# One written-out job order per engine for the even layer of a two-layer hybrid diffusion backbone

## The reference

```python
def even_inputs(h, w_in, lb, qn_w, kn_w):
    qa, zf, zb, ia, ga, qb, kb, vb = split_cols(h @ w_in, EVEN_SIZES)
    q_r = rec(jax.nn.silu(qa), DK_A) * (DK_A ** -0.5)
    g_f = jnp.log(lbf[0] + (1.0 - lbf[0]) * jax.nn.sigmoid(rec(zf, DK_A)))   # g_b from zb likewise
    v_r, gate = rec(ia, DV_A), ga.reshape(b, l, H_A, DV_A)
    q_a = rms_norm(qb.reshape(b, l, H_B, HD_B), qn_w)
    k_a = rms_norm(kb.reshape(b, l, KV_B, HD_B), kn_w)
    v_a = vb.reshape(b, l, KV_B, HD_B)

def even_layer_lat(h, p, j, lbs, k_ctx, v_ctx, s_ctx):     # the context tokens likewise
    o_r, _ = hgrn_bidir(q_r, g_f, g_b, v_r, s0[:, 0], s0[:, 1])        # mixer A, 4 heads
    out_a = hgrn_readout(o_r, gate, p['hgrn_norm_w'][j])               # rms_norm(o) * silu(gate)
    out_b = swa_latent_attention(rope_2d(q_a), rope_2d(k_a), v_a, k_ctx, v_ctx, p['swa_sink'][j])
    return jnp.concatenate([out_a, out_b], -1) @ p['w_out_even'][j]
```

## Time and profile before

| | |
|---|---|
| median of 3 runs | 1167.46 us |
| profiled execution, its own time | 1167.8 us |
| its span (first to last instruction) | 1165.7 us |
| PE busy | 1054.6 us, 90% |
| DVE / ACT busy | 571.7 us, 49% / 486.8 us, 42% |
| first tile of unit 2 starts | 64.47 us |
| first tile of unit 15 starts | 338.71 us |

### The profile page before, as it was taken

How to read it: one execution, slowest core, us unless ns; L and a number is a source line. 1 busy time by engine, 2 the same in 40 slices (tenths; PEclk the granted TensorE clock), 3 DMA queues, 4 the chain that set the end, 5 groups by cost and what they waited for, 6 DMA issues and landing times.

```text
span 1165.7 us, 17989 instructions
## 1 busy us (share of the span) xinstructions
PE 1054.6 (90%) x7330; PEld 963.1 (83%) x7330; DVE 571.7 (49%) x906; ACT 486.8 (42%) x858; POOL 144.5 (12%) x170
## 2 busy tenths in 40 slices
PE   5798677788889999999996998999789999999998
PEld 2686455667789999999996987777579999999997
DVE  2543535655346544445456535555645544445452
ACT  4345344434435425243343535555535414334241
POOL 0051101000010102010013123113000101011010
PEclk9999898899999999999999999999889999999999
DMA  8865333366462443434332444443213343434321
GB/s 284 279 200 207 109 109 109 112 238 208 149 222 81 137 145 109 144 109 136 116 129 90 144 155 144 145 150 120 83 39 107 123 138 109 138 111 140 110 72 55
DMA packets 157099, 160.38 MB, mean 138 GB/s; under 512 B 3627, under 2 KB 155717, under 8 KB 157029
## 3 DMA queue, kind: packets, MB, share of 16 engines
q1 hardware_dynamic: 155028, 156.50, 40.9%
q0 software_dynamic: 528, 1.70, 0.4%
q10 hardware_dynamic: 1472, 1.18, 0.3%
HBM read 156.09 MB, written 3.28 MB: 137 GB/s over the span
## 4 chain that ended last, share of the span: by engine, by line
PE 76%; ACT 12%; DVE 7%; issue 4%; DMA 0%; SPq 0%; ACTq 0%; DVEq 0%
PE G L589 54%; PE G L594 10%; ACT wH L1040 3%; PE OB L612 3%; PE TB L563 3%; DVE wL L1493 1%; PE OB L946 1%; PE OB L792 1%; PE TB L612 1%; DVE small L1731 1%; PE SC L632 1%; DVE nbuf L1529 1%; ACT hq L1187 1%; PE SC L675 1%; PE SC L681 1%
## 5 line engine op out<-in xcount | busy, mean ns | idle before, releaser
L589 PE MATMUL G<-opH,wH 128*128 128x386 f32 (+1 forms) x768 | 273.2, 356 | 5.5 <-DVE wL L1493 3.1
L589 PE MATMUL G<-opH,wL 128*128 128x386 f32 (+1 forms) x768 | 264.8, 345 | 0.0
L589 PE MATMUL G<-opL,wH 128*128 128x386 f32 (+1 forms) x768 | 264.7, 345 | 0.0
L1040 ACT ACTIVATE wH<-raw 128x2048 fp32r<-128x2048 f32 x96 | 183.3, 1910 | 186.8 <-PE G L589 182.7
L1493 DVE TENSOR_TENSOR wL<-raw,wH 128x2048 fp32r<-128x2048 f32 x96 | 221.1, 2303 | 80.9 <-ACT wH L1040 80.9
L589 PE MATMUL G<-hidH,wH 128*128 128x384 f32 x512 | 172.5, 337 | 0.0
L589 PE MATMUL G<-hidH,wL 128*128 128x384 f32 x512 | 172.1, 336 | 0.0
L589 PE MATMUL G<-hidL,wH 128*128 128x384 f32 x512 | 172.1, 336 | 0.0
L589 PEld LDWEIGHTS G<-opH,wH 128*128 128x128 f32 x768 | 148.6, 194 | 16.9 <-issue 8.5
L589 PEld LDWEIGHTS G<-opL,wH 128*128 128x128 f32 x768 | 148.4, 193 | 0.9
L589 PEld LDWEIGHTS G<-opH,wL 128*128 128x128 f32 x768 | 148.4, 193 | 0.0
(11 more groups left out here) (244 smaller groups left out, 1161.5 us busy)
## 6 DMA issues: line engine op xcount, KB each, us to landing
raw<-in_w_mlp SPq DMA_DIRECT2D x64, 1024.0 KB, 5.2
raw<-in_w_ada SPq DMA_DIRECT2D x48, 1024.0 KB, 6.3
raw<-in_w_in_even SPq DMA_DIRECT2D x13, 1024.0 KB, 6.5
raw<-in_w_in_odd SPq DMA_DIRECT2D x12, 1024.0 KB, 5.0
raw<-in_w_out_even SPq DMA_DIRECT2D x4, 1024.0 KB, 5.3
raw<-in_w_out_odd SPq DMA_DIRECT2D x4, 1024.0 KB, 5.2
xin<-in_x_sample SPq DMA_DIRECT2D x1, 1024.0 KB, 6.4
out_y_sample<-yout SPq DMA_DIRECT2D x1, 768.0 KB, 4.0
```

The source lines that it names most:

```text
L589: mm = pe.matmul(G[:, s, 512 * m:512 * m + cols], w[:, s, k, P * m:P * m + P], a[:, k, 0:cols], start=first and q == 0, stop=last and q == 2)
L1040: act.activation(wH[:, u % 2, :, :], raw[:, pos % RAW, :, :], ACT.Copy).then_inc(w_high, 1)
```

## The change

The table of slots goes. In its place stand three lists, one each for PE, ACT and DVE, in which every job of units 2 to 14 (on PE to 16) is named one by one. `u4.25` is tiles 2 to 5 of unit 4. The first lines of the PE list and a stretch of each list from the middle:

```diff
-    for s in range(N_SWA + 3):
-        if s >= 2:
-            put(31 + 3 * s, f"swaA{s}")
-        if s < N_SWA + 2:
-            put(33 + 3 * s, f"swaB{s}")
...
+EVEN_PE = """
+    ada8 u2.04 adt8 ada9 u2.56 adt9 u2.77 u3.04 ada10 u3.56 adt10 ada11 tq0 u3.77 adt11 u4.00 tq1 u4.11 ada12 tk u4.25
...
+    tpb1 sc3 u8.33 adt19 u8.47 hg10 pv1 tpa2 u9.01 tpb2 sc4 pv2 tpa3 u9.23 tpb3 u9.44 sc5 u9.56 pv3 tpa4 u9.77 hg12
+    u10.04 hg14 tpb4 ada20 u10.55 adt20 ada21 u10.67 hg1 adt21 ada22 sc6 adt22 ada23 pv4 adt23 hg3 tpa5 ada30 tpb5 sc7
+    adt30 pv5 tpa6 tpb6 ada24 sc8 adt24 pv6 u11.01 ada25 hg5 u11.22 adt25 u11.33 ada31 tile0 turned0 u11.44 hg7 u11.56
...
+    tpb11 tile1 turned1 pv11 adt29 state1 hgN0 u14.02 hgO2 hgN1 u14.33 hgO3 hgN2 u13.01 ada33 hgN3 u13.23 adt33 ada34
+    u13.46 adt34 ada35 u13.77 adt35 u14.47 u15.07 u16.07
...
+EVEN_ACT = """
...
+    ada20 ada21 mix3 ada22 ada23 ex6 es6 pv4 tpa5 ada30 tpb5 mix5 sp11 tpa6 pv5 ex7 tpb6 es7 ada24 pv6 ex8 es8 ada25
...
+EVEN_DVE = """
+    masks sp2 ev0 sp3 rs0 ev1 adt8 rs1 adt9 sp4 ev2 rs2 adt10 adt11 sp5 ev3 adt12 mx0 adt13 sp6 share0 mx1 ev4 share1
...
+    mx3 adt19 sp9 share3 hg10 grow10 ev8 mx4 hf1 share4 mx5 sp10 hg12 grow12 share5 ev9 hg14 grow14 ins0 ks1 adt20 hg1
```

```diff
-        mx, negm, dsink = small[:, 64:66], small[:, 66:68], small[:, 68:70]
+        mx, negm = small[:, 64:66], small[:, 66:68]
+        dsink = small[:, 72:76].rearrange("p (i c) -> p i c", c=2)
...
+            def gate_sigmoid(u):
...
                 act.wait_ge(g_free[u % 2], u // 2 + 1)
                 settle(act.activation(f, f, ACT.Ln, bias=ones[:, 0:1]))
                 act.activation(f, f, ACT.Exp, scale=-1.0).then_inc(sig_set, 1)
...
-                act.activation(esink[:, s % 2, :], dsink, ACT.Exp).then_inc(exp_set, 1)
+            def swa_sink(s):
+                act.activation(esink[:, s % 2, :], dsink[:, s % 2, :], ACT.Exp).then_inc(exp_set, 1)
...
-                if s:
-                    dve.wait_ge(exp_set, s)
-                dve.tensor_tensor(dsink, sk, mx, ALU.subtract)
+                dve.tensor_tensor(dsink[:, s % 2, :], sk, mx, ALU.subtract)
```

More of the change, by code:

```diff
@@ new lines @@
+""".split()
+EVEN_ACT = """
+    sp2 ev0 ev1 sp3 rs0 ada8 ada9 rs1 sp4 ev2 rs2 ada10 ada11 tq0 ev3 sp5 tq1 eb3 ada12 tk ada13 ex0 sp6 ev4 es0 eb4
+    ada14 ex1 es1 ev5 ada15 tpa0 sp7 mix2 ev6 eb6 ada16 tpb0 mix4 ex2 ada17 es2 sp8 tpa1 pv0 mix6 ev7 eb7 ada18 mix8
+    ada19 tpb1 mix10 sp9 ex3 es3 ev8 tpa2 pv1 tpb2 mix12 pv2 tpa3 ex4 tpb3 es4 sp10 ex5 ev9 pv3 tpa4 es5 mix14 tpb4
+    ada20 ada21 mix3 ada22 ada23 ex6 es6 pv4 tpa5 ada30 tpb5 mix5 sp11 tpa6 pv5 ex7 tpb6 es7 ada24 pv6 ex8 es8 ada25
+    mix7 ada31 tile0 turned0 sp12 mix9 ev11 ev10 hgO0 tpa7 mix11 ada26 tpb7 pv7 ex9 es9 ada27 tpa8 tpb8 mix13 pv8 ex10
+    tpa9 es10 sp13 hgO1 tpb9 pv9 ex11 es11 ada32 tpa10 tpb10 state0 mix15 ev12 ada28 pv10 tpa11 sp14 tpb11 ada29 tile1
+    turned1 pv11 swo0 swo1 swo2 state1 hgN0 swo3 hgH0 hgO2 hgN1 hgO3 hgH1 hgN2 ada33 hgH2 hgN3 hgH3 ada34 ada35
@@ L166, in psum_uses @@
         ob.append(f"ada{a}")
[L168 to L202, removed]
-    even_jobs(EVEN_TAIL)
+    for name in EVEN_PE:
+        kind, i = job(name)
+        if kind in ("hg", "tq", "tile"):
+            sc.append(name)
+        elif kind == "sc":
+            sc.append(f"swa{i}")
+        elif kind == "adt":
+            tb.append(f"ada{i}")
+        elif kind in ("tk", "turned", "hgN"):
+            tb.append(name)
+        elif kind in ("tpa", "tpb"):
+            tb.append(f"swaP{i}.{kind == 'tpb':d}")
+        elif kind in ("ada", "state", "hgO"):
+            ob.append(name)
+        elif kind == "pv":
+            ob.append(f"swaO{i}")
     sc.append("norm1")
@@ L803, in even_jobs @@
                     kind, i = job(name)
-                    if kind == "hg":
+                    if kind.startswith("u"):
+                        u, tiles = name[1:].split(".")
+                        even_tiles(int(u), int(tiles[0]), int(tiles[1]) + 1)
+                    elif kind == "hg":
                         hg(i)
@@ L1233, in even_jobs @@
                         evict(i)
+                    elif kind == "eb":
+                        gate_sigmoid(i)
                     elif kind == "sp":
@@ L1303, in evict @@
                     act.activation(vout[:, :, :], g3[:, :, P:UC], ACT.Copy).then_inc(g_free[u % 2], 1)
-            for u in range(2, 13):
-                even_jobs(EVEN_JOBS[u])
-            even_jobs(EVEN_TAIL)
+            even_jobs(EVEN_ACT)
             for u in range(13, 17):
@@ L1757, in even_jobs @@
                         hg_pick(i)
+                    elif kind == "hf":
+                        hg_queries(i)
+                    elif kind == "ks":
+                        hg_keys(i)
+                    elif kind == "masks":
+                        block_masks()
+                    elif kind == "ins":
+                        hg_insert(i)
                     elif kind == "grow":
@@ L1804, in evict @@
                     qk_norm(swa_sq(u)[:, 0:HD * count], u, count)
-            for u in range(2, 13):
-                even_jobs(EVEN_JOBS[u])
-            even_jobs(EVEN_TAIL)
+            even_jobs(EVEN_DVE)
             scales(1, 20)
```

137 lines of the change are left out of this document (54 added, 83 removed).

## The result

The changed kernel took 1098.92 us (median of 4 runs, 1096.58 to 1101.46), the kernel before beside it 1167.32 us: a ratio of 0.9427, 95% interval 0.9404 to 0.945. Forecast were 1124 us, 1109 to 1148. The profiled execution took 1101.46 us, the longest of the four.

A forecast was written before the change was run, and what follows sets the result against it. PE bounds the kernel, 90% busy; only its idle time and lower clock can be gained. Between units 2 and 15, work 203.1, idle 21.0 and clock 7 make 231.1 us instead of 274.3: 1124 us, range 1109 to 1148.

The forecast's parts named there:

- Work: Unit 2 to unit 15: full-speed PE work 208.0 us, less 4.9 for 49 fewer tile/small-job changes, gives 203.1 us.
- (a): PE's new list: nine distances too short even for idle helpers leave 3.8 us of idle time.
- (b): Between the transposes of `ada19` and `ada20`: DVE 90% full, some 24.5 of 27.5 us, costs PE 4 us idle.
- (c): Run of 21 small jobs between units 10 and 11: DVE surplus 3.7 us plus 1 for weights, 4.7 us idle.
- (d): Elsewhere in the stretch: 27.4 us of queues go; three quarters of the remaining 11.6, 8.5 us, stay.
- Clock: Unit 2 to unit 15: lower-clock excess falls from 16.5 to 7 us as idle time is cut by 58%.
- The sink's second buffer: Local attention: removes a DVE wait for ACT's previous sink exponential, worth 0 us alone.
- Behind unit 15: The 301 us behind the changed stretch: everything takes as long as before.
- 1 (lists that don't fit): Fixed lists mismatch the chip; half of 39 us of queues return and the clock costs 11: 1139 us; chance 0.18.
- 3 (round trip laid bare): Attention pairs from unit 8 on each expose 6.8 us of round trip and `SC` use: 1185 us; chance 0.05.
- 5: Better than forecast: DVE-full idle 1 us, queues elsewhere 2, clock 3, giving 1111 us; chance 0.17.
- 2 (the clock in the run of small jobs): Run before unit 11 goes at half clock, 12 us more, and some 3 in unit 12's tail: 1139 us; chance 0.06.

The follow-up runs named there:

- helper_lists_split_first: Kernel before with PE's order kept, ACT and DVE given own lists made for it, unit 2's split first: 1120.3 us, ratio 0.9597.
- vector_plus4: Changed kernel with four added reductions of 1.21 us each on DVE between `adt19` and `adt20`: 1097.6 us, ratio 0.9410.
- pauses: Changed kernel with five stops of PE put in, at the ends of units 3, 5, 7, 9 and 12: 1114.2 us, ratio 0.9552.
- sink_only: Kernel before with all three engines in its old order and only the two buffers of `dsink` added: 1165.4 us, ratio 0.9984.
- helper_jobs_joined: Changed kernel with the jobs it had divided on ACT and DVE joined again: 1101.0 us, ratio 0.9438.
- vector_plus8: Changed kernel with eight added reductions of 1.21 us each on DVE between `adt19` and `adt20`: 1103.0 us, ratio 0.9449.
- changed_again: Changed kernel unedited, measured once more beside the kernel before: 1098.9 us, ratio 0.9421.
- scalar_plus64: Changed kernel with 64 one-element copies added on ACT, one behind every second job: 1101.7 us, ratio 0.9439.
- pe_list_only: Changed kernel with its PE list kept and the helpers' lists replaced by PE's order: 1159.3 us, ratio 0.9922.

## Why the prediction was wrong

Its kind of argument held: queues were what PE waited for, the lists took them apart, the change reached the one stretch. Its sum did not. By its steps, for the stretch, 231.1 us forecast and 210.4 measured:

- **Work, 203.1 forecast, 205.5 measured.** helper_lists_split_first runs the old PE order at full clock with PE busy for 209.0 us, so the full-speed work of before was 209.0, not 208.0, and the clock's excess 15.5, not 16.5: both nearly right. The 49 fewer changes between tiles and small jobs gave 209.0 - 205.5 = 3.5 us, 0.07 each, not 4.9.
- **(a) Short distances, 3.8 forecast, 3.3 measured** of the 4.8 us that the list of waits adds up to. The other 1.5 are the two waits behind DVE's order, `tile1` and `tpa6`. Part of `tpb6`'s 1.0 is such a wait too: ACT copies `tpa6` only behind the split of unit 11.
- **(b) DVE full, 4 us forecast, 0 measured.** Wrong twice. DVE was busy for 21.4 us there, not 24.5, and of 28.5, not 27.5: the list has 18 tiles there, not 17, and `ins0` and `ks1` were done behind `adt20`'s place. So DVE was at 75%, below the 80% that the prediction wanted to see. And vector_plus4 shows that even 88% costs 0.5.
- **(c) The run of small jobs, 4.7 forecast, 2.2 measured** (16.60 - 14.41), of which `pv4` and `tpb6`, 1.5, are again (a), and `tpa6`, 0.6, is DVE's order. The weights were not late: the four pieces came in the 16.6 us at 324 GB/s, and ACT waits for no transfer there. DVE's surplus of 3.7 us over PE in part of it cost no more than that 0.6, since work may run late within the lists' slack.
- **(d) Queues elsewhere, 8.5 forecast, 1.0 measured (`tile1`). This is the step that failed.** Two kinds of wait were shown to be queues and counted as gone; three quarters of the other 11.6 us were kept, for the reason that both helpers would be busier, at 57% and 52%. The runs show that this reason has no force. DVE at 88% in one stretch, and ACT with 5.8 us more over all of it, leave PE's idle time at 5 us; whereas the same helpers at the load of before stopped PE for 40 us when one of them had the old order. Order, not load, made the waits. And the kinds do not add up one by one: the two lists are worth 9 and 16 us alone and 44 to 47 together.
- **Clock, 7 forecast, 0 measured in the stretch.** The excess was scaled with the idle sum. But 15.5 us of idle time cost nothing in helper_lists_split_first, 11.0 us of added stops cost 4.1 us in pauses, and the same 40 us or so cost about 11 us with ScalarE's list alone and 6 with VectorE's (PE busy 220.3 and 215.0, less 209.0 at full clock; some 2 of the 11 are at the start, behind the faulty head). The longest stop that the changed kernel had left is 1.0 us. Longer stops in the forecast came with (b) and (d).
- **The sink's second buffer, 0.** sink_only agrees.
- **Behind unit 15, no difference forecast, 4.3 us measured**, in span (827.0 to 822.7), and PE busy fell by 4.3 (786.2 to 781.9) with the same instructions. It is the clock. Of before, 30.6 us behind unit 15 are at half clock, in five pieces; in the changed kernel 20.4, in three of 6.8 (the last 4 us, low in both, left aside). Below, the three pieces of before that went or shrank, then the place of the last of them in the changed kernel:

```profile
339.50:342.90 3.40, 3.40 (x13) 3.40 (x12) 3.40 (x5) 0.94 (x2) 0.00 (x0) 0.50 0.90 266
704.70:708.10 3.40, 2.93 (x13) 2.93 (x14) 2.46 (x5) 1.18 (x7) 0.00 (x0) 0.50 0.89 297
636.40:646.60 10.20, 5.78 (x27) 5.81 (x28) 10.02 (x20) 4.00 (x10) 3.33 (x1) 0.50 0.30 103
```
```profile
571.50:578.30 6.80, 2.99 (x14) 3.02 (x15) 6.69 (x12) 2.41 (x6) 2.72 (x1) 0.50 0.42 137
578.30:581.70 3.40, 3.40 (x36) 3.06 (x39) 3.33 (x11) 1.61 (x4) 0.00 (x0) 1.00 0.12 39
```

The first of them followed the 2.3 us wait before unit 15, which the changed kernel does not have. For the others no cause is shown.

In sum 2.4 - 16.1 - 7 - 4.3 = -25.0 us, and 1124 - 25 = 1099. That this meets the median to the microsecond is luck: the sum is of the profiled executions, the changed kernel's took 1101.5 us and lies 1.9 us further above its span than that of before, and the median is 2.5 us under it.

**The rivals.** 1 (lists that don't fit): no. 3 (round trip laid bare): no, attention's waits are under 1.1 us each. 5 was nearest, and right in its direction; it too kept 11.5 us idle and 3 of clock. 2 (the clock in the run of small jobs) needs a closer look. In the changed kernel that run is at 1.00 with 14.4 us busy in 16.6, so it is not the 12 us that the rival named. But helper_jobs_joined and vector_plus8 each had 3.4 us at half clock in this run and nowhere else in the stretch:

```profile
185.90:189.30 3.40, 3.40 (x23) 1.36 (x16) 1.99 (x5) 1.60 (x7) 0.00 (x0) 0.51 0.26 62
```

(helper_jobs_joined; the other's row is above.) It followed stops of 0.57 and 0.99 us, and with the same stops there the changed kernel, changed_again, vector_plus4 and scalar_plus64 kept 1.00; helper_lists_split_first kept 1.00 behind single stops of 1.3 and 1.6 us among tiles. The Trainium skill (TensorE: Matmul & The Clock Gate, Part 4: PE-mode transpose) says that a transpose "doesn't count as PE-busy the same way". Transposes are only 4.2 of the 14.4 us that PE is busy in this run, the rest are matmuls, so the run is no test of that rule, and the prediction took too much from it when it let the whole run go slow. That this run is nearer to a fall than others, the two kernels suggest. What decides between falling and not there is open.

**What PE's own list is worth** beside the helpers' is at most the difference between helper_lists_split_first and the changed kernel, 21 us by the medians. In the traces it is 10.6 us less idle and 3.5 less work in the stretch, and 7.2 behind unit 15 (829.9 to 822.7), where again only the clock differs, 0.97 to 0.99. The 14.1 us of the stretch are the list's own. The 7.2 cannot be put down to it: pe_list_only, which has the same PE list, takes 830.0 us behind unit 15, while the seven other traces of kernels with the changed kernel's three lists or nearly so take 823.1 to 823.9, and pauses 825.7. Why the later part runs at different clocks with the same instructions was not tried and stays open.

## What to carry to other kernels

Where three engines share one job order, give each its own, and judge the change by all of them at once: lists changed one at a time gave 8, 9 and 16 us, and the two helpers' together 44 to 47, since a chain through both moves much of its wait. When a forecast sorts waits into queues and short distances, let a fitted order take nearly all the queues, and keep the distances: here the distances kept 3.3 us and the queues 1.5. A helper's busy share is no ground for a wait by itself: 88% over 29 us cost 0.5 us here. Do not scale the clock's price with the idle sum; look at the single stops that remain, and keep a few microseconds of doubt, since short ones were twice followed by a fall.
